# Experts of a decoder step in turns of a 160-row and a 128-row block, with bounded row transfers

## The reference

```python
def route(h, w_router, router_bias):
    scores = jax.nn.sigmoid((h @ w_router).astype(F32))
    sel = scores + router_bias.astype(F32)
    # keep the 4 best of 8 groups of experts, then the 8 best of 64 experts
    _, eidx = lax.top_k(sel, TOP_K)
    w = jnp.take_along_axis(scores, eidx, axis=1)
    return eidx, w / jnp.sum(w, axis=-1, keepdims=True) * ROUTED_SCALE

def swiglu(x, wg, wu, wd):
    return (jax.nn.silu(x @ wg) * (x @ wu)) @ wd
# each token: x + shared swiglu + sum over its 8 experts of weight * swiglu of that expert
```

## Time and profile before

| | us |
|---|---|
| median of 3 runs | 2243.35 (2241.21 to 2246.22) |
| profiled execution | 2233.79 |
| its span | 2232.0 |
| PE busy in the span | 2087.2 (94%) |

### The profile page before, as it was taken

One profiled execution on the slowest core, in us unless ns is written; L12 is line 12 of the kernel. 1 busy time (PEld: TensorE's weight loads), 2 busy tenths in 40 slices (PEclk: granted clock), 3 DMA queues, 4 the chain that ended last, 5 costly groups with the idle time before them and its releaser, 6 DMA issues. The chain is left out here.

```text
span 2232.0 us, 42929 instructions
## 1 busy us (share of the span) xinstructions
PE 2087.2 (94%) x15302; PEld 1576.0 (71%) x15302; DVE 1342.0 (60%) x2337; ACT 1049.4 (47%) x1608; POOL 1028.9 (46%) x850
## 2 busy tenths in 40 slices
PE   7999889968799989999898989999999999999994
PEld 6777667746444458888687647777777777777773
DVE  4488767685676661111367437777777777677772
ACT  6321223276666651111233116666666666666662
POOL 2111223252687730110016515676766767667662
PEclk9999999989899999999999999999999999999997
DMA  6488811073645538891533268999999999999996
GB/s 225 154 272 259 265 56 39 27 247 106 229 155 162 188 134 288 273 303 48 177 123 97 81 270 293 339 340 334 330 339 339 339 335 331 341 339 338 330 331 155
DMA packets 178690, 520.62 MB, mean 233 GB/s; under 512 B 22907, under 2 KB 77354, under 8 KB 152142
## 3 DMA queue, kind: packets, MB, share of 16 engines
q1 hardware_dynamic: 130070, 355.43, 45.1%
q0 software_dynamic: 37520, 97.81, 17.1%
q10 hardware_dynamic: 10992, 66.02, 8.7%
HBM read 442.31 MB, written 125.08 MB: 254 GB/s over the span
## 5 line engine op out<-in xcount | busy, mean ns | idle before, releaser
L2740 DVE TENSOR_TENSOR w_gu_lo<-turned,w_gu_hi 128x2048 fp32r<-128x2048 f32 x132 | 302.7, 2294 | 146.5 <-ACT w_gu_hi L2662 146.5
L2662 ACT ACTIVATE w_gu_hi<-turned 128x2048 fp32r<-128x2048 f32 x132 | 253.9, 1924 | 39.4 <-PEq L1942 39.4
L641 PE MATMUL pP<-wring,hT_hi 128*128 128x512 f32 (+1 forms) x576 | 225.8, 392 | 18.5 <-DVE wring L567 11.4
L643 PE MATMUL pP<-wring,hT_lo 128*128 128x512 f32 (+1 forms) x576 | 221.2, 384 | 0.0
L642 PE MATMUL pP<-wring,hT_hi 128*128 128x512 f32 (+1 forms) x576 | 220.9, 384 | 0.0
L2589 PE MATMUL pG_e<-w_gu_hi,xT_hi 128*128 128x512 f32 x528 | 215.5, 408 | 0.0
L2589 PE MATMUL pG_e<-w_gu_lo,xT_hi 128*128 128x512 f32 x528 | 209.9, 398 | 0.0
L2589 PE MATMUL pG_e<-w_gu_hi,xT_lo 128*128 128x512 f32 x528 | 209.3, 396 | 0.0
L2516 POOL DMA_INDIRECT x_scratch<-turned,target x66 | 106.8, 1619 | 198.8 <-ACT turned L2703 198.8
L2502 POOL DMA_INDIRECT turned<-h_scratch,index x64 | 167.5, 2617 | 20.0 <-issue 20.0
L399 POOL TENSOR_TENSOR wring<-turned,wring 128x512 fp32r<-128x512 f32 (+1 forms) x43 | 67.5, 1594 | 228.9 <-ACT wring L433 228.6
(11 more groups left out here) (336 smaller groups left out, 4991.2 us busy)
## 6 DMA issues: line engine op xcount, KB each, us to landing
turned<-in_w_e_up SPq DMA_DIRECT2D x65, 1024.0 KB, 11.3
turned<-in_w_e_down SPq DMA_DIRECT2D x65, 1024.0 KB, 6.8
turned<-in_cache_sb_kv SPq DMA_DIRECT2D x256, 256.0 KB, 3.1
turned<-in_w_e_gate SPq DMA_DIRECT2D x64, 1024.0 KB, 7.2
out<-in_cache_win_kv ACTq DMA_DIRECT2D x8, 4094.0 KB
turned<-in_w_in ACTq DMA_DIRECT2D x56, 256.0 KB, 6.1
turned<-in_w_in SPq DMA_DIRECT2D x16, 512.0 KB, 7.3
out<-in_cache_win_kv ACTq DMA_DIRECT2D x8, 1022.0 KB
```

The source lines that it names most:

```text
L641: pe.matmul(pP[:m, i % 4, :w], hi, w_hi(u), start=(c == 0), stop=False)
L643: last = pe.matmul(pP[:m, i % 4, :w], lo, w_hi(u), start=False, stop=(c == KC - 1))
L2662: act.activation(ghi[:, r, k, :, :].rearrange("p c f -> p (c f)"), w[:, r, k, :], ACT.Copy).then_inc(ghi_ready, 1)
L2740: dve.tensor_tensor(glo[:, r, k, :, :].rearrange("p c f -> p (c f)"), w[:, r, k, :], ghi[:, r, k, :, :].rearrange("p c f -> p (c f)").bitc ...
```

## The change

A turn now has a first block of up to 160 rows (`LONG` = 0) and a second of up to 128 (`SHORT` = 1). An expert's last block counts as long if it has more than 128 rows. The list has all long blocks first and then the short ones; the first half of the list goes to the long places, the second to the short ones, and the number of turns is the larger of half of all blocks, rounded up, and the number of long blocks. A short block that stands in a long place has a tail of unused slots. The table is gathered in units of 32 rows, five of them for each block, with five indirect DMAs, and a short block's fifth unit points to an unused one.

In the expert stage all steps of the tail are dropped for the second block of a turn, and the order of `body` is written out for the pair. PE turns the next long block's rows before gate and up of the short block, and the short block's between tail and gate and up of the long one. The loads' waits are changed to suit. All indirect gathers and scatters of the stage get a bound (`bounds_check`, `oob_is_err=False`): a row number behind the last token is skipped. `y` gets a second buffer, so that `put` waits for the scatter of two blocks before; the scatter itself still waits until the one before has landed. POOL copies the target numbers ahead of the gather, no longer behind it. Cut to its core:

```diff
+TAIL = BLK - P
+UNITS = BLK // TAIL
 TURN = 2
-NBLK = -(-((T * TOPK + E * (BLK - 1)) // BLK) // TURN) * TURN
-SLOTS = NBLK * BLK
+NBLK = 128
...
-    tail = [flat[:, at + r * (D // QT):at + (r + 1) * (D // QT)] for r in range(2)]
+    tail = flat[:, at:at + D // QT]
     at = KC * T + 4 * D + DE // P * T
     rows.append(flat[:, at:at + D])
     at = 6 * KC * DE
-    y = flat[:, at:at + D]
+    y = [flat[:, at:at + D]]
     y_tail = flat[:, at + D:at + D + D // QT]
+    at = KC * T + 9 * D + P
+    y.append(flat[:, at:at + D])
...
-                pool.indirect_dma_start(table, None, by_block, bass.IndirectOffsetOnAxis(ap=where[:NBLK, 0:1], axis=0)).then_inc(table_in, 16)
+                for q in range(UNITS):
+                    pool.indirect_dma_start(table[:, 2 * q * TAIL:2 * (q + 1) * TAIL], None, by_unit,
+                                            bass.IndirectOffsetOnAxis(ap=where[:NBLK, q:q + 1], axis=0)).then_inc(table_in, 16)
...
+                    longs, none = kinds[:, :E], float(UNITS * EXTRA)
+                    chain(dve.scalar_tensor_tensor(count[:, :], nblk[:, :], -float(P), count[:, :], ALU.mult, ALU.add))
+                    for j in range(CAP):
+                        chain(dve.scalar_tensor_tensor(longs, count[:, :], float(j * TAIL), longs, ALU.is_gt, ALU.add))
+                    chain(dve.tensor_tensor(kinds[:, E:], nblk[:, :], longs, ALU.subtract))
+                    chain(dve.tensor_tensor_scan(end[:, :], ones[:, :2 * E], kinds[:, :], 0.0, ALU.mult, ALU.add))
+                    long_blocks, blocks = end[:, E - 1:E], end[:, 2 * E - 1:]
+                    chain(dve.tensor_scalar(turn_used[:, :], turn_first[:, :], blocks, None, ALU.is_lt))
+                    chain(dve.tensor_reduce(turns[:, :], turn_used[:, :], AX_X, ALU.add))
+                    chain(dve.tensor_tensor(turns[:, :], turns[:, :], long_blocks, ALU.max))
+                    dve.tensor_scalar(expert_row[0:1, NBLK:], turns[0:1, :], -2.0, None, ALU.add).then_inc(row_ready, 1)
...
+                    for q in range(UNITS - 1):
+                        dve.tensor_scalar(where[:, q:q + 1], unit, none + q, None, ALU.add)
+                    dve.tensor_scalar(where[:, UNITS - 1:], rest, -1.0, none + UNITS - 1, ALU.mult, ALU.add).then_inc(where_ready, 1)
...
                 def load_gate_up(it, j):
                     e = expert(it, j)
                     if seen(it, j, 2):
-                        sp.wait_ge(gut_ready, it * U + (j - 1))
-                        sp.nop(nofuse=True)
+                        if j == LONG:
+                            sp.wait_ge(gut_ready, it)
+                            sp.nop(nofuse=True)
                         sp.wait_ge(glo_ready, it * (2 * U) + (2 * j - 2))
                     for k in range(2):
                         if seen(it, j, 2 - k):
-                            load(e, j % 2, k)
+                            load(e, j, k)
 
                 def load_down(it, j):
                     e = expert(it, j)
                     if seen(it, j, 2):
-                        sp.wait_ge(y_ready, it * U + (j - 1))
-                    load(e, j % 2, 2)
+                        if j == LONG:
+                            sp.wait_ge(y_ready, it * U - 1)
+                        else:
+                            sp.wait_ge(wlo_ready, it * U)
+                    load(e, j, 2)
 
                 def body(it):
-                    for j in range(U):
-                        if seen(it, j, 1):
-                            load_gate_up(it, j)
-                        if seen(it, j, 2):
-                            load_down(it, j - 1)
+                    if seen(it, LONG, 1):
+                        load_gate_up(it, LONG)
+                        load_down(it - 1, SHORT)
+                    load_gate_up(it, SHORT)
+                    if seen(it, LONG, 1):
+                        load_down(it, LONG)
                 body(0)
                 last = load_last(sp)
                 with sp.Fori(1, last + 1) as it:
                     body(it)
-                load_down(last, U - 1)
-                sp.wait_ge(y_out, last * (U * 32) + U * 32)
+                load_down(last, SHORT)
...
                 def gather(it, j):
-                    r = j % 2
-                    if seen(it, j, 2):
-                        pool.wait_ge(x_psum, it * (3 * U) + 3 * (j - 1))
-                    pool.tensor_copy(index[:, r, :], slot_info[:, bass.ds(it * U + j, 1), 0:2]).then_inc(index_ready, 1)
+                    pool.wait_ge(x_psum, it * 5 if j == SHORT else it * 5 - 2)
+                    pool.tensor_copy(index[:, j, :], slot_info[:, bass.ds(it * U + j, 1), 0:2]).then_inc(index_ready, 1)
                     pool.wait_ge(index_ready, it * U + (j - 1))
                     pool.nop(nofuse=True)
-                    pool.indirect_dma_start(rows[r], None, sc["h2"], bass.IndirectOffsetOnAxis(ap=index[:, r, 0:1], axis=0)).then_inc(rows_in[r], 16)
-                    pool.indirect_dma_start(tail[r], None, h2_quarters, bass.IndirectOffsetOnAxis(ap=index[:, r, 1:2], axis=0)).then_inc(rows_in[r], 16)
+                    pool.indirect_dma_start(rows[j], None, sc["h2"], bass.IndirectOffsetOnAxis(ap=index[:, j, 0:1], axis=0),
+                                            bounds_check=T - 1, oob_is_err=False).then_inc(rows_in[j], 16)
+                    if j == LONG:
+                        pool.indirect_dma_start(tail, None, h2_quarters, bass.IndirectOffsetOnAxis(ap=index[:, j, 1:2], axis=0),
+                                                bounds_check=QT * T - 1, oob_is_err=False).then_inc(rows_in[j], 16)
 
                 def aim(it, j):
 
-                    pool.tensor_copy(target[:, j % 2, :], slot_info[:, bass.ds(it * U + j, 1), :]).then_inc(target_ready, 1)
+                    pool.tensor_copy(target[:, j, :], slot_info[:, bass.ds(it * U + j, 1), :]).then_inc(target_ready, 1)
 
                 def scatter(it, j):
 
-                    r = j % 2
                     pool.wait_ge(target_ready, it * U + (j + 1))
-                    pool.wait_ge(y_copied, it * (2 * U) + 2 * (j + 1))
                     if seen(it, j, 1):
-                        pool.wait_ge(y_out, it * (U * 32) + 32 * j)
+                        pool.wait_ge(y_out, it * 48 + 32 * j)
+                    pool.wait_ge(y_copied, it * 3 + 2 * (j == SHORT) + 1)
                     pool.nop(nofuse=True)
-                    pool.indirect_dma_start(sc["x2"], bass.IndirectOffsetOnAxis(ap=target[:, r, 0:1], axis=0), y, None,
-                                            compute_op=ALU.add).then_inc(y_out, 16)
-                    pool.indirect_dma_start(x2_quarters, bass.IndirectOffsetOnAxis(ap=target[:, r, 1:2], axis=0), y_tail, None,
-                                            compute_op=ALU.add).then_inc(y_out, 16)
+                    pool.indirect_dma_start(sc["x2"], bass.IndirectOffsetOnAxis(ap=target[:, j, 0:1], axis=0), y[j], None,
+                                            bounds_check=T - 1, oob_is_err=False, compute_op=ALU.add).then_inc(y_out, 16)
+                    if j == LONG:
+                        pool.wait_ge(y_copied, it * 3 + 2)
+                        pool.nop(nofuse=True)
+                        pool.indirect_dma_start(x2_quarters, bass.IndirectOffsetOnAxis(ap=target[:, j, 1:2], axis=0), y_tail, None,
+                                                bounds_check=QT * T - 1, oob_is_err=False, compute_op=ALU.add).then_inc(y_out, 16)
 
                 def body(it, old):
                     for j in range(U):
+                        if old is not None:
+                            aim(old, j)
                         if seen(it, j, 2):
                             gather(it, j)
                         if old is not None:
-                            aim(old, j)
                             scatter(old, j)
...
                     for f in range(NF):
-                        pe.transpose(hT[:, f, :], hid[:, f, :], ident[:, :])
-                    for h in range(2):
-                        last = pe.matmul(gT[64 * h:64 * h + 64, :, :], hid_q[:, :], pick[:, h], start=True, stop=True)
+                        last = pe.transpose(hT[:, f, :], hid[:, f, :], ident[:, :])
+                    if j == LONG:
+                        pe.wait_ge(hid_q_ready, it + 1)
+                        for h in range(2):
+                            last = pe.matmul(gT[64 * h:64 * h + 64, :, :], hid_q[:, :], pick[:, h], start=True, stop=True)
...
                 def body(it, which):
-                    for j in range(U):
-                        turn_next = which != "last" or j < U - 1
-                        if turn_next:
-                            turn_tail(it, j + 1)
-                        gate_up_tail(it, j)
-                        if turn_next:
-                            turn_rows(it, j + 1)
-                        gate_up(it, j)
-                        if which != "first" or j > 0:
```

(28 more changed lines are left out.)

219 lines of the change are left out of this document (123 added, 96 removed).

## The result

The changed kernel takes 2188.58 us (median of 3 runs, 2180.11 to 2193.04) against 2243.35: a ratio of 0.975, 95% interval 0.970 to 0.980. The forecast was 2168 us with a range of 2122 to 2208, so the direction and the range held, and 20.6 us were missing. The profiled run took 2188.58 us for a span of 2186.8, 45.2 less than the one of before.

The account below looks back on a forecast made before the run. The prediction took PE as the bound before and DMA after. From the median 2243.35 us, -72 for 33 turns, -3 for early turns, +3 for the table and -3 at the end gave 2168 us, range 2122 to 2208.

Parts of the forecast that it names:

- What bounded the kernel before: Expert stage: PE never waits and is the bound; DMA keeps up with nothing to spare, at a share of 1.01.
- 33 turns, and PE's sum of 22.88: Expert stage: turns stay 33; PE's work a turn falls from 26.48 to 22.88 us, 23.05 with a new weights wait.
- POOL and the weighted rows: Expert stage: the scatter wait moves from ACT to POOL; the scatter chain takes 20 us a turn, so no change.
- DMA sets the turn at 24.3: Expert stage: DMA limits the turn to 24.3 us, saving 2.18 us a turn, 72 over 33; chance 0.33.
- Early turns, 3 us: Start of the expert stage: a few turns run at PE's pace until weight loads fall behind; 3 us saved once.
- first engines gain nothing: Rival: DMA engines owning low partitions skip no first rows, so a turn takes 25.2 us; 2198 us, chance 0.24.
- The PE rival: Expert stage: DMA has slack that the share hides, so PE stays the bound; 2127 us, chance 0.27.
- The POOL rival: Expert stage: bounds make each indirect transfer 1.84 us dearer, so POOL sets the turn at 27.3 us; 2267 us, chance 0.04.
- The signs: Expected profile: PE gaps of 1 to 1.5 us a turn, 335 to 350 GB/s, q0 about 30%; wrong if turns exceed 25.
- Table, +3: Before the experts: five table gathers in place of one delay the shared expert's second half; 3 us more (0 to 5).
- The end, -3: Last block: its copy no longer waits for the scatter before, thanks to its own buffer; 3 us less (0 to 4).
- Sum: Whole kernel: all terms together take 75 us off, from the profiled 2233.8 to 2158.8, from the median to 2168 us.

Follow-up runs that it names:

- e9: The changed kernel run again without edits, on one chip with versions that scatter into two arrays: 2185.14 us, ratio 0.971 to the kernel before.
- e5: The kernel before with only the bounds added to the expert stage's gathers and scatters: 2238.31 us, ratio 0.9994.
- e4: The changed kernel with long and short blocks scattered into separate arrays, gather first on POOL, nine residual reloads dropped, sums added at the end: 2177.71 us, ratio 0.970.
- e10: The version of e4, bounds kept, run again on the chip of e9: 2176.20 us, ratio 0.968 to the kernel before.
- e12: The version of e4 with bounds on the scatters only, none on the gathers: 2174.15 us, ratio 0.967 to the kernel before.
- e11: The version of e4 without bounds, as in e6, run again on the chip of e9: 2172.17 us, ratio 0.968 to the kernel before.
- e8: The version of e4 with nearly 1 MB of the short block's gate weights a turn not loaded, results wrong: 2149.63 us, ratio 0.961.
- e7: The kernel before with its table of slots fetched by five gathers of 32 rows in place of one of 160: 2239.72 us, ratio 1.0006.
- e6: The version of e4 with the bounds taken off, so padding rows move again: 2164.71 us, ratio 0.968 to the kernel before.

## Why the prediction was right, and where it was not

The direction, the 33 turns and PE's sum were right by their reasons. That the turn came near the forecast 24.3 and the time into the range was in part luck: 24.69 was set by a chain that the prediction had put out of play, and in e9 the same kernel has 25.08, past the prediction's own sign of being wrong ("over 25").

- **What bounded the kernel before: right.** PE alone. e5 took 23 GB/s of traffic away and gained nothing.
- **33 turns, and PE's sum of 22.88, with the short block's weights 23.05: right.** 22.97 in every undisturbed turn. The new wait for the low weights, 0.15 by the working, can't be more than 0.09.
- **POOL and the weighted rows: this is the step that failed.** The text had the scatter chain at "1.9 + 9.1 + 9.1", 20 us, "under 24". The dependence was seen and every term of it was too small. From start to start the slow turn at 1604.57 has 2.8 between the long block's two scatters (1.9 in the sum), 11.8 from the second of them to the next block's scatter (9.1) and 13.2 from that one to the next (9.1): 27.8 us, more than any other term. The 9.1 of the earlier trace rows counts from the start of the issue and holds an issue of 1.6; here the two issues are 1.9 and 3.1 and what follows them 10.0 and 10.1. Why the landings are longer no view names. e4 shows what the chain costs by taking it away: 24.69 to 23.68. "Behind it on POOL are the next row numbers' copy and gather, for a block nearly a turn away": the gather did come late, up to 4.2 us, as one waiting instruction holds POOL for nearly 6 and nearly 8 us in such a turn.
- **DMA sets the turn at 24.3: the next bound, not the first, and its size nearly right by two errors.** Late turns of e4 and e10 have 23.8 to 23.9 us. But the working read a share of 1.01 at 336 GB/s as full. It was not: 370 were to be had. And it credited the bounds with 1.2 us a turn (25.5 to 24.3), where e10 to e12 show none. They have opposite signs. The term behind both is the weights' "16.74" us a turn, which was held fixed: it is 15.9 in e10 and 15.2 in e11, so it gives way to POOL's packets. POOL's own terms came nearly as worked out, 8.1 with bounds (8.06) and 9.0 without (9.27).
- **Early turns, 3 us: too small.** In e4 ten turns ran at PE's pace while a lead was eaten; at some 0.9 us each that is 9 us.
- **The rival "first engines gain nothing"** had the mechanism that fits what bounds did: bytes fall, the rate falls with them (336 to 313 GB/s in e5, 369 to 355 from e11 to e10), the turn stays. That it is a matter of which engine owns which partitions no row shows; that stays open. Its level, 25.2 us, shared the wrong ceiling.
- **The PE rival, 2127 us:** its turn is what e8 reaches, but only with a sixth of the weights left out.
- **The POOL rival, "2267":** by its own terms (+27, -3, +3) it is 2270. It didn't come: in e5 the bounded transfers take POOL what the unbounded ones took before (the row scatter 1.62 us in both, the tail gather 2.80 and 2.83).
- **The signs.** PE's gaps were there, but they ended with the gather and not with DVE's low parts. The rate was in the range named (335), q0 at 34.0% and not 30%. The count of q0's packets misled: some 763 a turn point to rows that are not skipped by the text's measure ("some 600 if rows are skipped"), but a skipped row leaves a small packet.
- **Table, +3: too much.** e7 has +1.3, not visible in the time. The longer chain of counts on DVE cost nothing, as the gather still waited last for the scatters of the table.
- **The end, -3: too much.** Behind PE's last product the kernel is 1.2 us shorter (27.6 to 26.4).
- **Sum.** The 33 turns gave 64.0 instead of 72 and 3 for the early ones, the end 1.2 instead of 3: near 13 us short. The start, +20 instead of +3, is 17 more; to judge by e5 to e8, hardly 1 of them belongs to the change. The profiled execution of before was itself 9.6 us under its median, so against the medians not all of this shows: 54.8 us of the 75 forecast came.

## What to carry to other kernels

When an edit moves a wait onto an engine that also issues other work, add up the whole cycle of that wait: every issue in it at the length it has under load, every landing, and ask which instructions stand behind it. A share of DMA near 1.0 says that packets are under way, not that no more fit (1.01 at 332 GB/s before, 1.03 at 370 in e6). Nor is the engines' time for a given transfer a fixed price that can be added up: the weights' fell from 16.7 to 15.2 us a turn as the turns grew shorter. Before bytes are saved, find out whether the transfer that sets the pace gets any shorter by it.

## What the hardware showed that was not expected

- A PE that had idled for 3.9 us came back at a granted clock of 0.58 for 4.1 us, at a cost of 1.3 us on top of the wait. Waits of this size cost a third more than they measure.
- The changed kernel, with two limits close together (chain and DMA), runs in groups of turns: several at 22.97, then several at 24 to 28. In a slow turn the DMA share falls, to 0.80 in the window above. That the lead is built again there, and so the groups come about, is a reading and not shown.
- A scatter's issue on POOL is not constant. Before, all 66 of L2516 took 1.57 to 1.64 us; behind a wait for a landing the changed kernel's L2548 takes 1.57 to 3.53. What lengthens it no run here shows. The copies of row numbers took 0.18 to 1.35 us in the turns above.
- Skipped rows cost next to no bytes and still gave no time, at 311 as at 352 GB/s, and the weights' packets beside them took longer: 66.2% of the engines' time for 154.20 MB in e5, 63.2% for 154.31 before.
